# A two-layer hybrid decoder trunk with a mixture of experts: feature-major residual, more expert buffers, a shorter router chain, unrolled layers

## The chip, the cores and the metric

The kernel runs on one core of one Trainium2 chip. The metric is the device time of one execution in microseconds (us), as a median over runs; less is better. TensorE (PE in the profile) multiplies, VectorE (DVE), ScalarE (ACT) and GpSimd (POOL) work on elements, SyncE (SP) issues nearly all DMAs.

## The reference

The input is 256 tokens of 1024 features in fp32. Each of two layers does the following, and a final RMSNorm ends it:

```
h = rms_norm(x, norm_mix)
proj = h @ w_in                       # 1024 x 4120
y = [gated DeltaNet (6 heads) | retention (4) | mLSTM (6)], chunks of 64 in the reference
x = x + y @ w_out                     # 1024 x 1024
tok = rms_norm(x, norm_ffn)
group = top-1 of softmax(tok @ router_group)              # 4 groups
e1, e2 = top-2 of (tok @ router_expert + bias) in the group  # 8 experts each
weights = softmax(top two logits) * group probability
for e in range(32):
    y = (silu(tok @ gate[e]) * (tok @ up[e])) @ down[e]     # 1024 x 256, 1024 x 256, 256 x 1024
    out = out + combine[:, e] * y
x = x + out
```

An expert has three weight matrices of 1 MiB. One layer's experts are 96 such matrices, and every one is read in every layer.

## The kernel before

All of it is one function, `trunk`, with one program per engine; the engines meet by semaphores. The residual `x` lies token-major in SBUF: 128 partitions are tokens, two tiles `j` of 128 tokens, 1024 features along the free dimension. `hT` holds the normed input with features on partitions, in eight slices `k` of 256 tokens. Slice `k` holds every eighth feature from `k` on.

**A layer, in order.** (1) DVE scales `x` to `xn` (L1251), PE transposes it (L507), DVE evacuates with the gain (L1258) to `hT`. (2) The mixer: the projection is split into 20 weight slots (`PROJ`; `gatesT` at L523 is the first, the others go through L477 and L492), between them the work of the heads. (3) `project_out` (L784) multiplies by `w_out` in four parts `n`; DVE adds each to `x` (L1540, semaphore `x_mixed`). (4) The router: `x` is transposed (L834), `logitsT` is computed (L842), transposed back (L850), scaled by the row norm (L1559), then DVE picks group and experts in small instructions, each waiting for the one before (`link`). PE counts ranks (`rank`, L863 to L866); DVE builds `Psel`, a 0/1 matrix that picks 32 tokens for each of four experts (L1608). (5) The expert phase.

**Expert phase.** A quad is four experts. A round on PE is: gate matmuls of the quad (L912), transposed weights of the chosen tokens (L920), up matmuls (L912), the gather of the next round's tokens (`gather`, L881), transposes (L933), down matmuls (L942), and the combine into PSUM banks 0 to 3 (L953), where the residual has been put before by identity matmuls (L857). Eight quads, and a quad with more than 32 tokens for an expert gets another round (`nround`); the profiled execution has nine rounds in each layer. The gather must be exact in fp32: the normed tokens are split into three bf16 parts `part[0..2]` by ACT and POOL (L1192, L422, L1197, L425), and each is multiplied by `Psel`, 48 bf16 matmuls of 128x128.

**Loads.** SP issues each weight load in program order after waiting for `slots_free`, which PE raises when it has read a buffer. w_in and w_out take 24 loads in a ring of 12 buffers of 1 MiB. Experts take 96 loads in 16 buffers: the 12 of the ring and 4 (`SPARE`) in `shared`, memory that the mixer uses too. Loads come as gate, up, down of a quad, four each.

**Between layers.** The layers are a loop on each engine (`Fori(0, LAYERS)`); quads are a loop as well. At a layer's end all engines meet (`end_of_layer`), and POOL clears the layer's semaphores and lets them go on (L433). DVE copies the sums from PSUM to `x` (L1675), ACT squares them (L1219, L1222) for the next norm.

## Time and profile before

| what | value |
|---|---|
| median of 3 runs | 1034.73 us (1033.13 to 1035.6) |
| the profiled execution's own time | 1033.16 us |
| its span, first to last instruction | 1031.4 us |
| PE busy | 859.6 us (83%) |
| DVE busy | 347.2 us (34%) |
| ACT busy | 216.8 us (21%) |
| POOL busy | 23.0 us (2%) |
| mean granted TensorE clock | 0.939 |
| moved by DMA | 249.42 MB, mean 242 GB/s |

What lies around the span is 1.8 us. Busy time is an average over stages that have different limits: for each stage one reads which wait ended last.

### The profile page before, as it was taken

Reading aid. Unit: us, or ns where it says so; the run is one execution under the profiler, and the core shown is the slowest. Engines: PE = TensorE matmul, PEld = TensorE weight load, DVE = VectorE, ACT = ScalarE, POOL = GpSimd, SP = SyncE. Lnnn points to the kernel's source line nnn. Section 1 sums busy time; section 2 is a strip of 40 time slices with the busy share of each in tenths; the row PEclk is TensorE's granted clock in tenths of the full one; section 3 lists DMA queues with packets and bytes.
Section 4 is the critical chain, followed back from the end, with each engine's and each line's share of the span. In section 5 each row is a group of like instructions: output and inputs, shape, how many; then the busy total and the mean of one; then the engine's idle time right before and its main releaser. Section 6 shows DMA issues by size and latency. Waiting matters only on the chain.

```text
span 1031.4 us, 18112 instructions
## 1 busy us (share of the span) xinstructions
PE 859.6 (83%) x6932; PEld 617.0 (60%) x6933; DVE 347.2 (34%) x773; ACT 216.8 (21%) x410; POOL 23.0 (2%) x26
## 2 busy tenths in 40 slices
PE   4999999989588867698679999999896877879665
PEld 3877887968354433444358778879674544445332
DVE  1656634424621111111126565344346111111112
ACT  1243222222311100011103442133123111111111
POOL 1000000000300000000000000000003000000000
PEclk9999999989899888899879999999998998989888
DMA  9913012534459999979955120134344799899993
GB/s 343 350 57 103 1 42 82 167 119 163 169 244 419 421 420 421 421 323 421 403 207 183 42 82 1 45 119 163 107 172 157 306 420 421 337 423 419 420 421 138
DMA packets 48474, 249.42 MB, mean 242 GB/s; under 512 B 6096, under 2 KB 18560, under 8 KB 19344
## 3 DMA queue, kind: packets, MB, share of 16 engines
q1 hardware_dynamic: 47824, 246.91, 60.4%
q0 software_dynamic: 576, 1.43, 0.5%
q8 instruction: 58, 0.95, 0.4%
q14 instruction: 16, 0.13, 0.0%
HBM read 247.50 MB, written 1.05 MB: 241 GB/s over the span
## 4 chain that ended last, share of the span: by engine, by line
PE 50%; DMA 23%; DVE 12%; issue 7%; PEld 2%; ACT 2%; PEldq 1%; SPq 1%; DVEq 1%; POOLq 0%; ACTq 0%
PE ps L477 16%; DMA ring<-e_down 15%; PE ps L784 5%; PE ps L912 5%; PE ps L942 5%; DMA ring<-e_up 4%; PE ps L492 3%; PE ps L881 3%; DMA shared<-e_down 3%; DVE kq L1425 3%; DVE shared L1430 2%; PE ps L685 1%; PEld ps L912 1%; PE ps L639 1%; PE ps L953 1%
## 5 line engine op out<-in xcount | busy, mean ns | idle before, releaser
L477 PE MATMUL ps<-hT,ring 128*128 128x256 f32 x864 | 191.0, 381 | 0.0
L477 PEld LDWEIGHTS ps<-hT,ring 128*128 128x128 f32 x864 | 162.7, 190 | 25.9 <-issue 2.5
L912 PE MATMUL ps<-ring,hT 128*32 128x256 f32 x1728 | 114.7, 424 | 43.0 <-DMA ring<-e_up 21.7
L912 PEld LDWEIGHTS ps<-ring,hT 128*32 128x32 f32 x1728 | 67.2, 122 | 90.6 <-issue 69.8
L881 PEld LDWEIGHTS ps<-kq 128*128 128x128 bf16 x960 | 65.0, 149 | 10.0 <-issue 7.4
L953 PE MATMUL ps<-hT,kq 128*128 128x512 f32 x144 | 66.1, 602 | 5.5 <-PE ps L942 5.5
L881 PE MATMUL ps<-kq 128*128 128x128 bf16 x960 | 67.9, 235 | 2.3 <-DVE kq L1608 2.3
L1608 DVE TENSOR_TENSOR kq<-shapes,sel 128x128 bf16<-128x128 f32 (+1 forms) x40 | 9.9, 288 | 156.0 <-PE ps L920 155.7
L942 PE MATMUL ps<-ring,kq 128*32 128x512 f32 x448 | 51.0, 595 | 13.1 <-DMA ring<-e_down 8.4
L784 PE MATMUL ps<-ring,xn 128*128 128x256 f32 x256 | 58.8, 385 | 0.0
L912 PE MATMUL ps<-shared,hT 128*32 128x256 f32 x576 | 39.8, 437 | 21.9 <-DMA shared<-e_up 20.4
L953 PEld LDWEIGHTS ps<-hT,kq 128*128 128x128 f32 x144 | 25.9, 189 | 47.2 <-issue 47.2
L784 PEld LDWEIGHTS ps<-ring,xn 128*128 128x128 f32 x256 | 48.6, 193 | 7.9 <-issue 1.3
L912 PEld LDWEIGHTS ps<-shared,hT 128*32 128x32 f32 x576 | 22.0, 126 | 39.7 <-issue 32.4
L1212 ACT ACTIVATE kq<-ps 128x256 f32<-128x256 f32 x18 | 6.9, 384 | 181.6 <-PE ps L933 181.6
L1669 DVE TENSOR_TENSOR kq<-kq,ps 128x256 f32<-128x256 f32 x18 | 7.6, 421 | 101.9 <-PE ps L912 101.9
L1625 DVE TENSOR_TENSOR hT<-ps,par 128x512 f32<-128x512 f32 x40 | 27.7, 692 | 36.9 <-PE ps L881 36.6
L1672 DVE COPY hT<-ps 128x512 f32<-128x512 f32 x18 | 12.4, 692 | 80.0 <-PE ps L942 80.0
L942 PEld LDWEIGHTS ps<-ring,kq 128*32 128x32 f32 x448 | 14.8, 109 | 39.2 <-issue 33.2
L1208 ACT ACTIVATE kq<-ps 128x256 f32<-128x256 f32 x18 | 6.9, 384 | 147.0 <-PE ps L912 147.0
L492 PE MATMUL ps<-ring,hT 128*128 128x128 f32 (+1 forms) x256 | 36.4, 302 | 0.0
L492 PEld LDWEIGHTS ps<-ring,hT 128*128 128x128 f32 x256 | 34.4, 191 | 2.2 <-issue 0.3
(303 smaller groups left out, 976.9 us busy)
## 6 DMA issues: line engine op xcount, KB each, us to landing
ring<-e_gate SPq DMA_DIRECT2D x48, 1024.0 KB, 21.8
ring<-e_up SPq DMA_DIRECT2D x48, 1024.0 KB, 10.8
ring<-e_down SPq DMA_DIRECT2D x48, 1024.0 KB, 23.6
ring<-w_mix SPq DMA_DIRECT2D x34, 1024.0 KB, 10.1
shared<-e_down SPq DMA_DIRECT2D x16, 1024.0 KB, 7.8
shared<-e_gate SPq DMA_DIRECT2D x16, 1024.0 KB, 18.7
shared<-e_up SPq DMA_DIRECT2D x16, 1024.0 KB, 26.5
ring<-w_mix SPq DMA_DIRECT2D x12, 512.0 KB, 7.2
```

The lines of the kernel that those rows point to most:

```text
L477: mm = pe.matmul(bank[:, ct * T:(ct + 1) * T], w[:, k, ct * P:(ct + 1) * P], hT3[:, k, :], start=(k == 0), stop=(k == KD - 1))
L492: mm = pe.matmul(bank[:, j * n:(j + 1) * n], hT3[:, k, j * P:(j + 1) * P], w[:, k, 0:n], start=(k == 0), stop=(k == KD - 1))
L639: mm = pe.matmul(bank[0:rows_, m * P + c0:(m + 1) * P], Amat[:, 4 * g + m, 0:rows_], XT[:, 4 * g + m, c0:P], start=True, stop=True)
L784: mm = pe.matmul(ps[:, b, j * COLS:(j + 1) * COLS], mixT[:, k, j * P:(j + 1) * P], w[:, k, :], start=(k == 0 and j == 0), stop=(k == KD - ...
L881: mm = pe.matmul(ps[:, 4 + 3 * half, kk * P:(kk + 1) * P], part[i][:, j, k:D:KD], Psel[:, j, :], start=(j == 0 and i == 0), stop=(j == TT ...
L912: mm = pe.matmul(ps[32 * e:32 * e + 32, 5 + m, 0:DE], hq[:, k, 32 * e:32 * e + 32], slot[at[e]][:, k * DE:(k + 1) * DE], start=(k == 0), s ...
L942: mm = pe.matmul(ps[32 * e:32 * e + 32, 5 + h, :], hmT[:, f, 32 * e:32 * e + 32], slot[at[e]][:, f * D + h * 512:f * D + (h + 1) * 512], s ...
L953: mm = pe.matmul(ps[:, 2 * j + h, :], PwT[:, j * P:(j + 1) * P], ysb[:, h, :], start=False, stop=False, skip_group_check=True)
L1425: link(TTn(diag(h), src, lvl[:, lev, :].unsqueeze(1).to_broadcast([P, 2, P]), ALU.mult))
L1430: link(TTn(XT[r_, 4 * g:4 * g + 4, c0:P], XT[r_, 4 * g:4 * g + 4, c0:P], bank.rearrange("p (m t) -> p m t", m=4)[r_, :, c0:P], ALU.subtract))
L1625: TTn(hq[:, half * 4:half * 4 + 4, :], ps[:, 4 + 3 * half, :].rearrange("p (k s) -> p k s", k=4), gq[:, half * 4:half * 4 + 4].unsqueeze(2 ...
L1672: dve.tensor_copy(ysb[:, 1, :], ps[:, 6, :]).then_inc(y1_ready, 1)
```

## The change

1. **Feature-major residual.** `xT` holds the residual with features on partitions (weights and outputs are permuted on the host to fit). The norm of the mixer sums squares over features by a matmul with a tile of ones (`ssq`), and DVE makes `hT` by one instruction per `k`. The transposes of `xn` go. `project_out` has weights stationary. In layer 1 the experts' sums gather feature-major in PSUM too, in layer 2 token-major for the output.
2. **19 load buffers for experts:** 12 of the ring, `S0` to `S3` in `shared`, `K` in `kq`, `L` (`late_buf`), `X` (the memory of `xT`, lent once the residual has been put in PSUM). A host-side `load_plan` writes down buffer and wait of each load.
3. **Router.** Logits from `xT` directly, with the group logits padded to 8 columns so that the maximum reads them in place; squares summed by matmuls into the same bank; indices compared without a cast; the mask of experts made from two small one-hot parts; what only the weights need stands behind the mask.
4. **fp32 gather:** `xn` comes from four transposes of `xT`, scaled by ACT; 16 fp32 matmuls of 128x128 instead of 48 bf16; POOL does nothing in it.
5. **Layers and quads unrolled, no barrier.** Semaphores count on (`upto`), POOL clears nothing. Parameters of both layers come in one DMA at the start; the constants' DMA stands behind the first three weight loads.
6. **Norm from PSUM:** at a layer's end ACT squares the sums in PSUM into 128x1024 halves, and the last norm reads PSUM as well.

```diff
+    ring, freed, count, landed, plan = list(range(RING)), {}, 0, {}, []
+    for _ in range(LAYERS):
+        wide = ring[0:8] + ["S0", "S3", "S1", "S2", "K"] + ring[8:12] + ["L", "X"]
+        gone = [ring[i % RING] for i in range(NPROJ)] + wide[8:]
+        gone += [wide[m % len(wide)] for m in range(NMOE)]
...
-    banks = [i % 8 for i in range(len(order))]
+    banks = [(i + 4) % 8 for i in range(len(order))]
...
         def _(sync):
-            sync.dma_start(shapes[:, :], consts).then_inc(const_in, 16)
-            with sync.Fori(0, LAYERS) as l:
+            for l in range(LAYERS):
                 for i in range(NMIX):
+                    b, need, _ = loads[l][i]
+                    if need:
+                        sync.wait_ge(slots_free, need)
+                    sync.dma_start(slot[b][:, 0:n], w_mix[l, i, :, 0:n]).then_inc(arrived[b], 16)
+                    if l == 0 and i == 2:
+                        sync.dma_start(shapes[:, :], consts).then_inc(const_in, 16)
...
         def _(pool):
-                for j in range(TT):
-                    pool.wait_ge(part_ready, j + 1)
-                    pool.tensor_tensor(rest[:, j, :], xn3[:, j, :], part[0][:, j, :], ALU.subtract).then_inc(rest_ready, 1)
-                for j in range(TT):
-                    pool.wait_ge(part_ready, TT + j + 1)
-                    pool.tensor_tensor(part[2][:, j, :], rest[:, j, :], part[1][:, j, :], ALU.subtract).then_inc(rest_ready, 1)
-                pool.wait_ge(layer_end, l * 4 + 4)
-                pool.sem_clear(per_layer)
-                pool.sem_inc(layer_go, 1)
...
         def _(pe):
-                transpose_x("hT", 0)
-                pe.wait_ge(hT_ready, 4)
+                bank = begin("ssq")
+                for i in range(2):
+                    pe.wait_ge(squared, upto(l, squared, i + 1))
+                    for k in range(4):
+                        mm = pe.matmul(bank[:, 0:T], ones[:, :], sq_in[:, 4 * (i if l == 0 else 1 - i) + k, :],
+                                       start=(i == 0 and k == 0), stop=(i == 1 and k == 3))
                 for k in range(KD):
+                    pe.wait_ge(hT_ready, upto(l, hT_ready, k + 1))
                     mm = pe.matmul(bank[0:NG, 0:T], slot_w(0)[:, k, 0:NG], hT3[:, k, :], start=(k == 0), stop=(k == KD - 1))
...
-                for i in range(4):
-                    j, half = i // 2, i % 2
-                    bank = begin(("h2T", i))
-                    pe.wait_ge(x_mixed, 4)
-                    for kk in range(4):
-                        mm = pe.transpose(bank[:, kk * P:(kk + 1) * P], x[:, j, half * 4 + kk:D:KD], c("ident"))
+                for n in range(4):
+                    pe.wait_ge(x_mixed, upto(l, x_mixed, n + 1))
+                    for k in (2 * n, 2 * n + 1):
+                        mm = pe.matmul(bank[0:NLOG, 0:T], rw[:, k, :], xT[:, k, :], start=(k == 0), stop=(k == KD - 1))
+                for n in range(4):
+                    pe.wait_ge(squared, upto(l, squared, n + 3))
+                    for k in (2 * n, 2 * n + 1):
+                        mm = pe.matmul(bank[64:96, 0:T], ones[:, 0:32], sq_mid[:, k, :], start=(k == 0), stop=(k == KD - 1))
...
+                for i in range(4):
+                    j, half_ = i // 2, i % 2
+                    bank = begin(("xt", i))
+                    for kk in range(4):
+                        mm = pe.transpose(bank[:, kk * P:(kk + 1) * P], xT[:, half_ * 4 + kk, j * P:(j + 1) * P], c("ident"))
...
+                pe.wait_ge(acc_init, upto(l, acc_init, 1))
+                pe.sem_inc(slots_free, 1)
...
                             for j in range(TT):
-                                for i in range(3):
-                                    mm = pe.matmul(ps[:, 4 + 3 * half, kk * P:(kk + 1) * P], part[i][:, j, k:D:KD], Psel[:, j, :],
+                                mm = pe.matmul(ps[:, 4 + 3 * half_, kk * P:(kk + 1) * P], xn3[:, j, k * P:(k + 1) * P], Psel[:, j, :],
...
-                with pe.Fori(0, QUADS // LAP) as mlap:
-                    for u in range(LAP):
+                for q in range(QUADS):
...
-                end_of_layer(pe, l)
...
         def _(act):
+                    act.activation(sq_in[:, 4:8, :], ps[:, 2:4, :].rearrange("p b (k t) -> p (b k) t", t=T), ACT.Square).then_inc(squared, 1)
+                    act.wait_ge(x_out, upto(l - 1, x_out, 1))
+                    act.activation(sq_in[:, 0:4, :], ps[:, 0:2, :].rearrange("p b (k t) -> p (b k) t", t=T), ACT.Square).then_inc(squared, 1)
+                link(act.activation(rstd_row[:, :], bank[:, 0:T], ACT.Ln, scale=1.0 / D, bias=epsc[:, :]))
+                act.activation(rstd_row[:, :], rstd_row[:, :], ACT.Exp, scale=-0.5).then_inc(rstd_ready, 1)
...
         def _(dve):
-                scale_x()
-                evac_hT("hT", "gain_mix")
+                for k in range(KD):
+                    dve.scalar_tensor_tensor(out=hT3[:, k, :], in0=xT[:, k, :], scalar=pv(l, "gain_mix", k), in1=rstd_row[:, :],
+                                             op0=ALU.mult, op1=ALU.mult).then_inc(hT_ready, 1)
...
-                link(dve.tensor_copy(rt[:, :, 30:31], rtx[:, 0, :, 0:1]))
-                link(dve.tensor_copy(rt[:, :, 48:50], rtx[:, 1, :, 0:2]))
-                link(TTn(rt[:, :, 59:60], rt[:, :, 41:42], rt[:, :, 40:41], ALU.subtract))
+                link(TTn(oh[:, :, 0:2, :], iota[:, 0:PER_GROUP].unsqueeze(1).unsqueeze(1).to_broadcast([P, TT, 2, PER_GROUP]),
+                         rtx[:, 1, :, 0:2].unsqueeze(3).to_broadcast([P, TT, 2, PER_GROUP]), ALU.is_equal))
+                link(TTn(oh[:, :, 2, :], oh[:, :, 0, :], oh[:, :, 1, :], ALU.add))
+                link(experts(0, 2))
                 dve.sem_inc(mask_ready, 1)
```

**DVE in the router.** First the rows of before, from the second group index to the two expert casts (`rt` is a small scratch tile, `rtx` the indices, `pick` the masks); then the rows after, as far as the mask of experts.

```order
L1568 MAX_INDEX rtx<-rt 128x8
L1569 CAST rt<-rtx 128x2
L1570 TENSOR_TENSOR rt<-rt 128x2x4
L1572 TENSOR_TENSOR rt<-shapes,rt 128x2x4
L1576 TENSOR_TENSOR pick<-lg,rt 128x64
L1577 TENSOR_REDUCE rt<-pick 128x2x8
L1579 MAX rt<-rt 128x8
L1580 MAX_INDEX rtx<-rt 128x8
L1579 MAX rt<-rt 128x8
L1580 MAX_INDEX rtx<-rt 128x8
L1581 CAST rt<-rtx 128x2x2
L1582 TENSOR_TENSOR rt<-rt 128x2
```

```order
L1538 MAX_INDEX rtx<-rt,lg 128x8
L1539 TENSOR_TENSOR rt<-shapes,rtx 128x2x4
L1543 TENSOR_TENSOR pick<-lg,rt 128x64
L1544 TENSOR_REDUCE rt<-pick 128x2x8
L1546 MAX rt<-rt 128x8
L1547 MAX_INDEX rtx<-rt 128x8
L1546 MAX rt<-rt 128x8
L1547 MAX_INDEX rtx<-rt 128x8
L1548 TENSOR_TENSOR oh<-shapes,rtx 128x2x16
L1550 TENSOR_TENSOR oh<-oh 128x2x8
L1554 TENSOR_TENSOR pick<-rt,oh 128x64
```

Both casts and the two subtractions are gone from ahead of the mask; before, five more instructions (L1585 to L1594) follow L1582 until the mask stands, and after none follows L1554.

**PE in the router,** from the last part of `project_out` to the first gather, before and then after (layer 1).

```order
L834 MATMUL ps<-shapes,x 128x128 x16
L842 MATMUL ps<-hT,rw 36x256 x8
L850 MATMUL ps<-shapes,lgT 128x128 x2
L857 MATMUL ps<-x,shapes 128x512 x4
L863 MATMUL ps<-pick,shapes 128x64
L864 MATMUL ps<-pick,shapes 128x64
L866 MATMUL ps<-pick,shapes 128x32
L357 ISA
L881 MATMUL ps<-kq 128x128 x48
```

```order
L822 MATMUL ps<-xT,rws 40x256 x8
L826 MATMUL ps<-hT,ones 32x256 x8
L831 MATMUL ps<-shapes,lgT 128x128 x2
L838 MATMUL ps<-shapes,xT 128x128 x16
L844 MATMUL ps<-xT,shapes 128x512 x4
L856 MATMUL ps<-pick,shapes 128x64
L857 MATMUL ps<-pick,ones 128x64
L859 MATMUL ps<-pick,ones 128x32
```

The 16 transposes moved from ahead of the logits to behind them, ahead of the rank; eight matmuls with ones are new. The gather follows as `L872 MATMUL ps<-kq,xn 128x128 x16`.

## Rows read from the trace of the kernel before

**Rows 1.** The page: the chain that ended last, shares of the span by engine.

```profile
PE 50%; DMA 23%; DVE 12%; issue 7%; PEld 2%; ACT 2%; PEldq 1%; SPq 1%; DVEq 1%; POOLq 0%; ACTq 0%
```

**Rows 2.** Windows: stretch, its length, busy time by engine, clock, DMA share, GB/s.

```profile
340.00:370.00 30.00, 21.42 (x232) 11.88 (x228) 3.48 (x8) 3.00 (x5) 0.00 (x0) 0.85 1.01 420
437.00:450.00 13.00, 11.71 (x114) 5.08 (x118) 1.09 (x3) 2.60 (x4) 0.00 (x0) 1.00 0.60 250
```

**Rows 3.** Timeline of SP's queue, expert loads: start, duration of issue, what.

```profile
293.10 2.07 SPq L395 DMA_DIRECT2D ring<-e_up  x4
...
449.20 2.19 SPq L395 DMA_DIRECT2D ring<-e_up  x4
...
805.03 2.09 SPq L395 DMA_DIRECT2D ring<-e_up  x4
```

**Rows 4.** Timeline of PE, expert phases of both layers; in brackets the idle time before.

```profile
437.44 3.64 PE L942 MATMUL ps<-ring,kq 128*32 128x512 f32 x32 [1.12 <-DMA ring<-e_down]
...
453.19 3.16 PE L881 MATMUL ps<-kq 128*128 128x128 bf16 x48
...
461.06 3.67 PE L953 MATMUL ps<-hT,kq 128*128 128x512 f32 x8 [0.30 <-PE ps L942]
464.66 3.66 PE L912 MATMUL ps<-shared,hT 128*32 128x256 f32 x64
...
492.94 5.12 PE L912 MATMUL ps<-shared,hT 128*32 128x256 f32 x64 [4.37 <-DMA shared<-e_up]
...
503.17 3.64 PE L942 MATMUL ps<-ring,kq 128*32 128x512 f32 x32 [1.71 <-DMA ring<-e_down]
507.10 3.67 PE L953 MATMUL ps<-hT,kq 128*128 128x512 f32 x8 [0.29 <-PE ps L942]
...
1014.39 3.64 PE L942 MATMUL ps<-ring,kq 128*32 128x512 f32 x32 [1.69 <-DMA ring<-e_down]
```

**Rows 5.** Timeline of PE in the first router.

```profile
261.46 2.00 PE L834 MATMUL ps<-shapes,x 128*128 128x128 f32 x16 [1.13 <-DVEq L1542]
264.25 3.62 PE L842 MATMUL ps<-hT,rw 128*36 128x256 f32 x16 [0.78 <-ACT hT L1183]
...
268.76 3.66 PE L857 MATMUL ps<-x,shapes 128*128 128x512 f32 x8
279.93 0.66 PE L863 MATMUL ps<-pick,shapes 128*128 128x64 f32 x2 [7.50 <-DVEq L1595]
...
282.55 5.32 PE L881 MATMUL ps<-kq 128*128 128x128 bf16 x48 [1.17 <-DVE kq L1608]
289.04 3.66 PE L912 MATMUL ps<-ring,hT 128*32 128x256 f32 x64 [1.16 <-DVE hT L1625]
```

**Rows 6.** Timeline of all engines in the same stretch: DVE and POOL.

```profile
268.96 0.55 DVE L1559 SCALAR_TENSOR_TENSOR lg<-ps,ss,par 128x36 f32<-128x36 f32 x2 [0.65 <-PE ps L850]
...
272.72 0.17 DVE L1570 TENSOR_TENSOR rt<-rt 128x8 f32<-128x8 f32 x1
...
274.21 4.20 POOL L425 TENSOR_TENSOR kq<-hT,kq 128x1024 bf16<-128x1024 f32 x2 [1.55 <-ACT kq L1197]
...
276.39 2.04 DVE L1582 TENSOR_TENSOR rt<-rt 128x2 f32<-128x2 f32 x1
```

**Rows 7.** The chain that ended last, in time, between the layers: start, duration, what.

```profile
510.83 1.24 DVE x L1675
...
514.53 6.10 issue
...
526.63 5.32 PE ps L523 x16
```

**Rows 8.** Timeline at the start: first projection matmuls.

```profile
16.43 3.62 PE L523 MATMUL ps<-hT,ring 128*24 128x256 f32 x16 [1.46 <-DVEq L1260]
```

**Rows 9.** The chain in time: 16 fp32 matmuls of 128x128 (two instructions each).

```profile
203.64 3.57 PE ps L492 x32
```

**Rows 10.** The page, costliest groups: busy us, mean ns of one, idle before.

```profile
L1212 ACT ACTIVATE kq<-ps 128x256 f32<-128x256 f32 x18 | 6.9, 384 | 181.6 <-PE ps L933 181.6
```

More of the change, by code:

```diff
@@ L46 @@
 RING = 12
-SPARE = 4
 SLOT = 2048
@@ L101, with load_plan @@
 LN_EXP = "natural_log_exp_and_others"
+def load_plan():
+    ring, freed, count, landed, plan = list(range(RING)), {}, 0, {}, []
[3 more added lines that the diff above has]
+        gone += [wide[m % len(wide)] for m in range(NMOE)]
+        turns = {b: [freed[b]] if b in freed else [0] for b in ring}
+        for b in gone:
+            count += 1
+            freed[b] = count
+            turns.setdefault(b, []).append(count)
+        loads = []
+        for b in [ring[i % RING] for i in range(NMIX)] + [wide[m % len(wide)] for m in range(NMOE)]:
+            landed[b] = landed.get(b, 0) + 16
+            loads.append((b, turns[b].pop(0), landed[b]))
+        plan.append(loads)
+        ring = sorted(ring, key=lambda b: freed[b])
+    return plan
 def psum_plan():
-    order = [("hT", i) for i in range(4)] + ["gatesT", ("gdn", 0), "gates"] + [("gdn", s) for s in range(1, 5)]
+    order = ["ssq", "gatesT", ("gdn", 0), "gates"] + [("gdn", s) for s in range(1, 5)]
     order += ["rows", "cols", ("gate", 0), ("beta", 0), ("beta", 1)] + [("nrm", s) for s in range(3)] + [("gate", 1)]
@@ L259, in trunk @@
         ps = ctx.enter_context(nc.psum_tensor("ps", [P, 8, 512], F32))
-        first = sem("layer_first")
-        full = [sem(f"bank_full{b}") for b in range(8)]
-        free = [sem(f"bank_free{b}") for b in range(8)]
+        full = [sem(f"bank_full{b}", uses[b]) for b in range(8)]
+        free = [sem(f"bank_free{b}", uses[b]) for b in range(8)]
         dve_chain = sem("dve_chain")
         act_chain = sem("act_chain")
-        rstd_ready = sem("rstd_ready")
-        squared = sem("squared")
@@ new lines, in _ @@
+                for b in range(4):
+                    pe.wait_ge(free[b], upto(l, free[b], uses[b]))
+                if l + 1 < LAYERS:
+                    for n in range(4):
+                        mm = pe.matmul(ps[:, n, :], c("ident"), xT[:, 2 * n:2 * n + 2, :], start=True, stop=False, skip_group_check=True)
+                else:
+                    for j in range(TT):
+                        for k in range(KD):
+                            mm = pe.matmul(ps[:, 2 * j + k // 4, k % 4 * P:(k % 4 + 1) * P], xT[:, k, j * P:(j + 1) * P], c("ident"),
+                                           start=(k % 4 == 0), stop=False, skip_group_check=True)
@@ L865, in _ @@
                           skip_group_check=True)
-                mm = pe.matmul(bank[:, 64:96], c("ones"), pick[:, 0, 1, :], start=False, stop=True, skip_group_check=True)
+                mm = pe.matmul(bank[:, 64:96], ones[:, :], pick[:, 0, 1, :], start=False, stop=True, skip_group_check=True)
                 done(mm, "rank")
-                for b in range(4, 8):
-                    if b != bank_of["rank"][0]:
-                        pe.wait_ge(free[b], uses[b])
+                for b in (4, 5, 7):
+                    pe.wait_ge(free[b], upto(l, free[b], uses[b]))
@@ L1185, in _ @@
-                x_square(1)
-                act.wait_ge(hT_ready_act, 2)
-                for i in (1, 3):
-                    act.sem_inc(free[bank_of[("h2T", i)][0]], 1)
-                rstd(rstd_ready)
-                for j in range(TT):
-                    act.wait_ge(xn_ready, 3 + j)
-                    act.activation(part[0][:, j, :], xn3[:, j, :], ACT.Copy).then_inc(part_ready, 1)
-                act.wait_ge(route_in, 1)
+                for n in range(4):
+                    act.wait_ge(x_mixed, upto(l, x_mixed, n + 1))
+                    act.activation(sq_mid[:, 2 * n:2 * n + 2, :], xT[:, 2 * n:2 * n + 2, :], ACT.Square).then_inc(squared, 1)
@@ L1194, in _ @@
+                act.wait_ge(route_in, upto(l, route_in, 1))
                 act.activation(rt[:, :, 24:28], rt[:, :, 20:24], ACT.Exp).then_inc(route_exp, 1)
[L1195 to L1198 removed]
+                act.wait_ge(route_in, upto(l, route_in, 2))
                 act.activation(rt[:, :, 60:61], rt[:, :, 59:60], ACT.Exp).then_inc(route_exp, 1)
[L1200 removed]
@@ L1201, in _ @@
-                act.sem_inc(first, 1)
-                with act.Fori(0, QUADS) as q:
-                    act.reg_load(nreg, nround[0:1, bass.ds(q, 1)])
+                act.wait_ge(routed, upto(l, routed, 1))
+                for q in range(QUADS):
+                    act.reg_load(nreg, nround[0:1, q:q + 1])
                     nv = act.snap(nreg, min_val=1, max_val=MAXROUND)
@@ L1653, in _ @@
                 selected(n0)
-                with dve.Fori(0, QUADS) as q:
-                    dve.reg_load(nreg, nround[0:1, bass.ds(q, 1)])
+                for q in range(QUADS):
+                    dve.reg_load(nreg, nround[0:1, q:q + 1])
                     nv = dve.snap(nreg, min_val=1, max_val=MAXROUND)
```

873 lines of the change are left out of this document (406 added, 467 removed).

## The prediction

> **What bounds the kernel now.** I read the page first: PE holds half of the chain that ended last, DMA 23% [rows 1]. Such shares mix stages, so I took windows next. In the expert phase the DMA engines run full at 420 GB/s while PE is busy for 21.42 of 30 us [rows 2]: there the weights set the pace, and PE waits for them (4.37 and 1.71 us near the end of layer 1) [rows 4]. In the mixer it is the other way round, PE and the short DVE and ACT steps between its matmuls; loads wait for buffers. Between the two lies the router, a serial chain in which DVE takes small steps and PE idles for 7.50 us ahead of the rank [rows 5]. So three things count: how many expert loads are left when the phase begins, when it begins, and what stands between and ahead of the layers.
>
> A model of the loads first. A load of 1 MiB at 420 GB/s takes 2.50 us [rows 2]. From an empty queue, 20 loads are issued from 449.20 on and the last lands at 503.17, where the down matmuls start [rows 3, 4]: 53.97 = 4.0 + 20 x 2.50. So a phase from its first reissue to its last landing costs 4.0 + 2.50 per load, if the queue never runs dry. Before, 16 of 96 loads are in at the start, 80 remain: 204.0. The trace has 503.17 - 293.10 = 210.1 in layer 1 and 1014.39 - 805.03 = 209.4 in layer 2. The 6.1 and 5.4 too many are a dry queue: at the quad with two rounds PE keeps the gate buffers until its second gate pass (one combine, 3.67, behind the down matmuls at 437.44, and 3.66 long), and only then is the next load issued, 449.20; DMA is busy for 0.60 of 437 to 450 [rows 2 to 4].
>
> **The parts.** The sum is made against the profiled execution, 1033.16 us, which is 1.6 under the median of 1034.73.
>
> *Three more buffers.* Loads left are 77: 4.0 + 192.5 = 196.5, if the queue doesn't run dry. Does it? The second gate pass of that quad (loads 60 to 63) frees what load 79 needs. The down loads of the first round (up to 72) land 4.0 + 53 x 2.50 = 136.5 after the first reissue; PE frees the gates 449.20 - 437.44 = 11.8 later, at 148.3; the queue comes to load 79 at 60 x 2.50 = 150 or later. It just doesn't run dry; in layer 2 the same distances hold for an earlier quad, with the same 2 us to spare. The loan of xT comes once the residual is in PSUM, some 11 us ahead of the first reissue (below), enough for its load. So DMA's end moves by 13.6 and 12.9 us against the first reissue.
>
> Then PE may set the end. From the landing at 437.44 to the combine's end at 510.77 it needs 73.33 [rows 4]. Off go its waits, 4.37 and 1.71, and nothing else; each of its three gathers gets dearer by 0.41 (next item): 68.5. In layer 1 that makes 136.5 + 68.5 = 205.0 after the first reissue; by the loads it is 196.5 + 7.60 = 204.1. Before it was 510.77 - 293.10 = 217.7. **Gain 12.7 in layer 1.** In layer 2 the long quad comes earlier and loads decide: (1014.39 + 7.60 - 805.03) - 204.1 = **12.9**.
>
> *The fp32 gather.* 48 bf16 matmuls take 3.16 us [rows 4]. No fp32 gather is in the trace; the nearest row is 16 fp32 matmuls of the same 128x128 shape, 3.57 [rows 9]: +0.41. Bounds: no dearer than bf16, or at half pace, 7.1. Inside the phase it hides in layer 2 behind 30 us of loads per quad.
>
> The Trainium skill (FP8 and Floating Point Precision, TensorE Precision Notes) says that true fp32 makes four passes through the array, so 64 passes against 48, which speaks against the change: by pass count 3.16 would become 4.2. The row agrees in sign, not in size; by the page the total would be some 2 us more.
>
> *The router.* Before, lg is done at 268.96 + 0.55 [rows 6]. After: project_out ends, as before, when x_mixed 4 comes, 261.3, just before the transposes at 261.46 [rows 5]. PE is free from about 260.4, so eight logit matmuls (3.62 [rows 5]) run behind the four adds and end near 264.0, eight matmuls with ones of that kind near 267.6. That is no gain on 267.87, where logitsT ended before: the transposes saved pay for the squares. Copy and transposes as before; ACT's Ln and Exp of a 2-column tile now stand between: lg at 269.9, 0.4 later.
>
> Then DVE. Here the rows show something odd: a 128x2 subtraction takes 2.04 us, and its kind takes 0.17; it ends at 278.43, as does POOL's 4.20 from 274.21 [rows 6]. From lg at 269.5 to the mask at 279.8 it is 10.3, far more than 20 such steps would need. POOL does nothing now, so what remains costs its small price, about 0.20 with its gap and 0.25 for 64 columns: maximum and index four pairs at 0.47, six other steps, semaphore 0.14: 3.4. The mask stands at 273.3 and not 279.8.
>
> That is the Trainium skill's rule in SBUF — State Buffer, Who interferes with whom: a VectorE instruction with two SBUF inputs, or in a two-port mode, is blocked for a whole GpSimd instruction. By it too, every such step falls to its own price once POOL is idle; the trace agrees (2.04 against 0.17).
>
> But PE isn't free for the rank at 273.3. Moved ahead of it are 16 transposes (2.00) and the residual's matmuls (3.66) [rows 5], from 268.7 on: until 274.4. *This is what is late next:* the rank waits 1.1 us for PE. From rank to gather took 282.55 - 279.93 = 2.62; one DVE step less: 2.4 [rows 5]. Gather at 276.9, at full pace 3.57: 280.5 (before it ran at 5.32 for the same 48 that took 3.16 later, after PE had idled). DVE's steps for the weights and rounds stand ahead of the evacuations, 17 of about 0.23 (two masks, nine for the weights, two to weigh, four for the rounds), 4.0 us from 276.85: so the first evacuation starts at 280.9, not with the gather's first half, and the gate starts at 281.9. Before 289.04 [rows 5]. **Gain 7.1 in each layer, 14.2.** Bounds: if the casts saved still cost (mixed types 1 us), 5; without the wait for PE, 8.5.
>
> *Between the layers.* Before: sums done 510.83, first projection 526.63 [rows 7]: 15.8, of which 6.10 is DVE waiting for nothing shown, after the barrier, at the loop's start. After, from the end of the sums: ACT squares one half (about 1.1), DVE copies the other (1.24 [rows 7]), then ACT squares that, done at 2.4; eight matmuls with ones, four after each half, 0.45 each (3.62 for eight [rows 8]): done at 4.8; Ln and Exp of 128x256, 0.38 each with gaps [rows 10]: 5.8; first slice by DVE 0.45: PE starts at 6.4. The slices come at PE's own pace. **Gain 9.4.** Bounds 3.3 (the 6.10 stays, in code that is new each time) and 10.
>
> *The start.* Before 16.43 [rows 8]; PE waits for constants until 11.50, then transposes. After: the input is in by about 6.5, squares to 7.6, ones matmuls to 9.8, Ln, Exp and the first slice 1.5: 11.3. **Gain 5.0.** The constants, now behind 2.2 MB of weights, come some 6 us later, near 18; the gate transposes that need them start at 22. If parameters or they come later still, this term shrinks, at worst to 0.
>
> *The end.* The final norm reads PSUM without the copy of the sums, 1.24 [rows 7]: **gain 1.2**.
>
> *Between these, at nothing:* the mixers have the same instructions; banks are shifted by one, which moves waits at project_out by less than a DVE step either way. Semaphores without clearing cost nothing.
>
> Sum: 12.7 + 12.9 + 14.2 + 9.4 + 5.0 + 1.2 = 55.4. 1033.16 - 55.4 = 977.8; against the median 979.3. I say 979.
>
> **Rivals.** (a) *TensorE becomes the bound.* The gather takes 7.1 instead of 3.57. PE's end in layer 1 moves by 3 x 3.5 = 10.5, and each router's gather by 3.5: 996. For it: PE and DMA are within 1 us of each other at the end of layer 1. Against: [rows 9]. 0.12.
>
> (b) *The buffers don't pay.* The queue runs dry elsewhere, or loans come too late, so that the phase starts earlier but isn't shorter: 979 + 25.6 = 1005. For it: only 2 us to spare at the long quad. Against: even with the old gap, 7.5 us of loads are gone in each layer. 0.08.
>
> (c) *Slower: straight code isn't there in time.* Quads, written out, are new to each engine. If entering each of the 16 quads cost the 6.10 us of [rows 7] on PE's way, 97.6 would be lost: 1077. It decides from 55.4 / 16 = 3.5 us per quad. Against: PE already walks through four quads of written-out code per pass of its loop, and goes from a quad's combine (461.06 + 3.67) to the next one's gate at 464.66 without a gap [rows 4]. 0.04.
>
> The Trainium skill (Runtime: NRT & Kernel Launch, Instruction fetch mechanics) says that fetch is sequential and hidden, and that a taken branch out of its window stalls; by it the 6.10 goes with the loop, and (c) doesn't happen. The row at 514.53 fits, no row here shows the fetch itself.
>
> (d) *More than I sum:* the mixers' waits shrink by the shifted banks and the tail of each phase goes at full clock: 966. 0.06.
>
> **The numbers.** My forecast 0.70. The range has to leave out 2 in 10: (c) and part of (b) above, part of (d) below, and must take in the bounds of the boundary (+6) and the router (+4) together with (a): 965 to 1001. This kernel's measurement can tell about 0.2% from no change. Faster by more holds in all cases but (c): 0.95; within 0.01; slower 0.04.
>
> **What the profile after would show.** Right: first reissue of expert loads near 281 in layer 1 (start 5.0 earlier, router 7.1), 196 to 197 us from there to the last landing in each layer, DMA share 1.0 all through, no stretch at 0.6; gather of 16 at about 3.6; PE idle ahead of the rank only shortly; DVE's small steps all under 0.3; 6.4 us from the end of layer 1's sums to the next projection. Wrong: a stretch with DMA idle inside the phase (the 79th load); PE without waits over the last quads (the bound has changed); idle ahead of each quad on any engine; a late parameter DMA at the start.

## The result and the profile after

The changed kernel takes 977.09 us (median of 4 runs, 975.59 to 980.22), the kernel before 1035.13 us next to it. The ratio is 0.9444, 95% interval 0.9425 to 0.9463. The prediction was 979.0 (965 to 1001): right in sign, in size and in the range. The profiled execution, the longest of the four, took 980.22 us with a span of 978.2 us; before it was 1033.16 and 1031.4.

The page of the changed kernel, busy time by engine and the chain that ended last:

```profile
PE 871.0 (89%) x6740; PEld 641.3 (66%) x6740; DVE 325.5 (33%) x756; ACT 192.5 (20%) x385; POOL 4.3 (0%) x15
...
PE 61%; DMA 17%; DVE 10%; issue 5%; ACT 3%; SPq 2%; PEld 1%; PEldq 1%; DVEq 1%; ACTq 0%
```

DMA's share of the chain falls from 23 to 17%, that of DVE and of issue too [rows 1]; PE gets most of it. Shares mix stages, so I cut both spans at the same events: first projection, first reissue of an expert load, end of the sums. The expert phase after, in windows (stretch, its length, busy time by engine PE to POOL, clock, DMA share, GB/s):

```profile
340.00:370.00 30.00, 20.65 (x213) 12.90 (x212) 3.48 (x8) 1.71 (x4) 0.00 (x0) 0.89 1.01 421
...
433.00:450.00 17.00, 16.09 (x170) 10.90 (x174) 3.48 (x8) 1.23 (x3) 0.00 (x0) 1.00 1.01 421
```

The stretch in which DMA had stood at 0.60 [rows 2] is gone: 1.01 at 421 GB/s. The first router and the start of the expert phase (timeline of all engines: start, duration, what; in brackets the idle time before):

```profile
267.89 0.55 DVE L1529 SCALAR_TENSOR_TENSOR lg<-ps,ss,pars 128x40 f32<-128x40 f32 x2 [1.18 <-ACT ss L1173]
...
269.05 3.60 PE L844 MATMUL ps<-xT,shapes 128*128 128x512 f32 x8
...
271.69 0.22 DVE L1554 TENSOR_TENSOR pick<-rt,oh 128x64 f32<-128x64 f32 x1
...
272.37 0.16 DVE L1562 TENSOR_TENSOR rt<-rt 128x2 f32<-128x2 f32 x1
...
272.77 0.33 SPq L405 DMA_DIRECT2D xT<-e_up  x1
272.95 0.41 PE L856 MATMUL ps<-pick,shapes 128*128 128x64 f32 x2 [0.30 <-PE ps L844]
...
274.71 3.84 PE L872 MATMUL ps<-kq,xn 128*128 128x128 f32 x32 [0.94 <-DVE kq L1573]
...
278.74 1.29 DVE L1590 TENSOR_TENSOR hT<-ps,pars 128x512 f32<-128x512 f32 x2
...
280.03 3.66 PE L900 MATMUL ps<-ring,hT 128*32 128x256 f32 x64 [1.48 <-DVE hT L1590]
...
284.09 0.33 SPq L405 DMA_DIRECT2D ring<-e_up  x1
```

From lg to the gate it is 280.03 - 268.44 = 11.6, where it was 289.04 - 269.51 = 19.5 [rows 5, 6]. PE no longer idles 7.50 us ahead of the rank but 0.30. The 128x2 subtraction that took 2.04 [rows 6] takes 0.16. The boundary between the layers, in the chain that ended last (start, duration, what):

```profile
489.17 1.03 ACT xn L999
490.20 0.14 issue
490.34 3.71 PE ps L499 x16
...
494.07 0.48 ACT rowsraw L1003
...
494.66 0.42 ACT rowsraw L1005
...
495.18 0.50 DVE hT L1264
...
495.81 3.61 PE ps L507 x16
```

The sums end at 489.17 and the projection starts at 495.81: 6.6 instead of 15.8 [rows 7], and no row of 6.10 is left. The start, on PE:

```profile
6.12 6.49 PE L499 MATMUL ps<-xn,ones 128*128 128x256 f32 x16 [6.12 <-ACT xn L996]
...
14.42 3.61 PE L507 MATMUL ps<-hT,ring 128*24 128x256 f32 x16 [1.82 <-DVE hT L1264]
```

Here is the one term that is much too small: 16.43 [rows 8] becomes 14.42, not 11.3. The same eight matmuls with ones (16 instructions) that take 3.71 between the layers take 6.49 here. What the trace of before shows at its start:

```profile
11.50 3.48 PE L507 MATMUL ps<-shapes,xn 128*128 128x128 f32 x16 [11.50 <-DMA shapes<-consts]
```

The router's 16 transposes of the same shape take 2.00 [rows 5].

| stretch | before | after | gain | predicted |
|---|---|---|---|---|
| to the first projection | 16.43 | 14.42 | 2.0 | 5.0 |
| mixer and router, layer 1 | 276.7 | 269.7 | 7.0 | 7.1 |
| first reissue to end of sums, layer 1 | 217.7 | 205.1 | 12.6 | 12.7 |
| between the layers | 15.8 | 6.6 | 9.2 | 9.4 |
| mixer and router, layer 2 | 278.4 | 269.7 | 8.7 | 7.1 |
| first reissue to end of sums, layer 2 | 217.0 | 205.1 | 11.9 | 12.9 |
| end | 9.3 | 7.6 | 1.7 | 1.2 |
| sum | | | 53.1 | 55.4 |

The spans differ by 53.2. The row for the mixer of layer 2 holds 1.7 us that the prediction had at nothing: before, the first projection of layer 2 took 5.32 us [rows 7] at a mean granted clock of 0.68 (526.63 to 531.95), behind 10.90 us in which PE was idle and 16 transposes at 0.50. Now it follows a short wait and takes 3.61 at 1.00.

### The profile page after: what moved, and what is told of

Same layout as the page of the kernel before. It is cut to its first block, busy times and chain, and to the rows that moved or that the text cites. A ratio compares the mean times of both kernels' runs of the same rounds, so it can differ in the third digit from the quotient of the medians.

```text
span 978.2 us, 16745 instructions
## 1 busy us (share of the span) xinstructions
PE 871.0 (89%) x6740; PEld 641.3 (66%) x6740; DVE 325.5 (33%) x756; ACT 192.5 (20%) x385; POOL 4.3 (0%) x15
## 4 chain that ended last, share of the span: by engine, by line
PE 61%; DMA 17%; DVE 10%; issue 5%; ACT 3%; SPq 2%; PEld 1%; PEldq 1%; DVEq 1%; ACTq 0%
PE ps L469 17%; PE ps L900 8%; PE ps L771 5%; PE ps L930 5%; PE ps L872 4%; PE ps L484 4%; DMA ring<-e_down 3%; DMA ring<-e_up 3%; DMA xT<-e_gate 3%; DVE kq L1402 3%; DMA shared<-e_down 3%; DMA late_buf<-e_up 3%; DMA ring<-e_gate 2%; DVE shared L1407 2%; SPq L405 2%
## 5 line engine op out<-in xcount | busy, mean ns | idle before, releaser
L469 PE MATMUL ps<-hT,ring 128*128 128x256 f32 x864 | 193.8, 384 | 0.0
L469 PEld LDWEIGHTS ps<-hT,ring 128*128 128x128 f32 x864 | 164.9, 193 | 26.7 <-issue 2.5
L872 PEld LDWEIGHTS ps<-kq,xn 128*128 128x128 f32 x640 | 73.0, 192 | 9.9 <-issue 7.4
L872 PE MATMUL ps<-kq,xn 128*128 128x128 f32 x640 | 76.8, 278 | 2.2 <-DVE kq L1573 2.2
L771 PE MATMUL ps<-xn,ring 128*128 128x256 f32 x256 | 58.0, 382 | 0.0
L771 PEld LDWEIGHTS ps<-xn,ring 128*128 128x128 f32 x256 | 48.0, 190 | 7.5 <-issue 1.0
L1590 DVE TENSOR_TENSOR hT<-ps,pars 128x512 f32<-128x512 f32 x40 | 27.5, 691 | 46.4 <-PE ps L872 46.2
L900 PE MATMUL ps<-kq,hT 128*32 128x256 f32 x128 | 33.2, 418 | 4.4 <-DMA ring<-e_up 4.1
L900 PE MATMUL ps<-late_buf,hT 128*32 128x256 f32 x144 | 36.1, 409 | 0.3 <-DMA ring<-e_gate 0.2
L942 PEld LDWEIGHTS ps<-kq,hT 128*128 128x128 f32 x144 | 26.6, 190 | 14.0 <-issue 10.8
L942 PE MATMUL ps<-kq,hT 128*128 128x256 f32 x144 | 33.3, 384 | 2.8 <-PE ps L930 2.8
L946 PE MATMUL ps<-hT,kq 128*128 128x512 f32 x72 | 33.1, 602 | 2.8 <-PE ps L930 2.8
```

Of the source, the lines that this page charges most:

```text
L469: mm = pe.matmul(bank[:, ct * T:(ct + 1) * T], w[:, k, ct * P:(ct + 1) * P], hT3[:, k, :], start=(k == 0), stop=(k == KD - 1))
L771: mm = pe.matmul(ps[:, b, i * T:(i + 1) * T], w[:, k, i * P:(i + 1) * P], mixT[:, k, :], start=(k == 0 and i == 0), stop=(k == KD - 1 and ...
L872: mm = pe.matmul(ps[:, 4 + 3 * half_, kk * P:(kk + 1) * P], xn3[:, j, k * P:(k + 1) * P], Psel[:, j, :], start=(j == 0), stop=(j == TT - 1))
L900: mm = pe.matmul(ps[32 * e:32 * e + 32, 5 + m, 0:DE], hq[:, k, 32 * e:32 * e + 32], slot[w[e][0]][:, k * DE:(k + 1) * DE], start=(k == 0), ...
L942: mm = pe.matmul(ps[:, k // 2, k % 2 * T:(k % 2 + 1) * T], ysb[:, h, k % 4 * P:(k % 4 + 1) * P], PwT[:, 0:T], start=False, stop=False, ski ...
L946: mm = pe.matmul(ps[:, 2 * j + h, :], PwT[:, j * P:(j + 1) * P], ysb[:, h, :], start=False, stop=False, skip_group_check=True)
```

## The experiments

All ratios are against the kernel before, run on the same chip beside each.

**Do the three lent buffers shorten the phase?** Take them out of the order of load buffers, with the releases that go with them:

```diff
-        wide = ring[0:8] + ["S0", "S3", "S1", "S2", "K"] + ring[8:12] + ["L", "X"]
+        wide = ring[0:8] + ["S0", "S3", "S1", "S2"] + ring[8:12]
```

> The changed kernel with K, L and X taken out of the experts' buffers: 16 as before. Nothing else differs. If loads set the end of the expert phase as the prediction has it, 80 loads are left at the first reissue, 4.0 + 200 us, and the queue runs dry at the quad with two rounds again (about 6 us): last landing 210 us after the first reissue, the sums complete at 217 to 218 instead of the 205.06 of the changed kernel, in both layers. In all 25 us more: about 1002, ratio to before 0.968. Rival, the buffers do not pay and the phase is only earlier: no change against the changed kernel, 0.944. Rival, only the dry queue goes and the three loads are hidden anyway: 12 us more, 0.956.

Measured: 998.63 us, 0.9646 (0.9628 to 0.9665), 21.5 over the changed kernel where 25 were expected; both rivals (0.944 and 0.956) are out. From the first reissue to the end of the sums it takes 497.23 - 279.55 = 217.7 us in layer 1 and 217.1 in layer 2, the lengths of the kernel before. So the buffers give 12.6 and 12.0, and the rest of the change nothing on balance within the phase. The total moved by less because the rest of this kernel was quicker: between the two profiled executions, 17.3 us apart, the first reissue comes 4.5 us earlier and the mixer of layer 2 takes 267.0 and not 269.7, and 12.6 + 12.0 - 4.5 - 2.7 is 17.4 (why, below). A second kernel gives two of the three back (K and L, not X, the residual's buffer):

> The changed kernel without the loan of xT's memory (X): 18 buffers. By the model 78 loads are left, 4.0 + 195 + 7.6 = 206.6 us from the first reissue to the end of the sums, against 205.06; the long quad had 2 us to spare and now none, so up to 1 us of a dry queue. Layer 1 +1.5 to 2.5, layer 2 +1.5 to 3.0: 3 to 5.5 us more in all, about 981, ratio 0.948. Rival, the loan comes too late to be of use: no change. Rival, TensorE alone sets the end of layer 1: only layer 2 gets longer, by 2.5.

Measured: 979.38 us, 0.9459 (0.9442 to 0.9476), only 2.3 over all three where 3 to 5.5 were expected. Its runs (979.04 to 979.58) lie within those of the changed kernel (975.59 to 980.22), so the phases have to decide. The phases are 489.21 - 281.03 = 208.2 and 206.8, against 205.1 each. So the third buffer is worth 3.1 us in layer 1 (1.5 to 2.5 were expected) and 1.7 in layer 2. The first two carry most, as they also nearly close the gap at the two-round quad: in layer 1 DMA is busy for 0.25 of 430 to 435 and 0.60 of 435 to 440 with 16 buffers, for 0.72 and 1.00 with 18, and for 1.02 and 1.01 with 19.

**Is it POOL's work that slows the router?** The kernel before, with POOL's four subtractions taken out. With them gone, ACT's second copy is scaled by 0 and the gather reads the second part twice, so the tokens are gathered in bf16 precision only; no instruction of another engine is left out:

```diff
-                    pool.tensor_tensor(rest[:, j, :], xn3[:, j, :], part[0][:, j, :], ALU.subtract).then_inc(rest_ready, 1)
+                    pool.sem_inc(rest_ready, 1)
...
-                                    mm = pe.matmul(ps[:, 4 + 3 * half, kk * P:(kk + 1) * P], part[i][:, j, k:D:KD], Psel[:, j, :],
+                                    mm = pe.matmul(ps[:, 4 + 3 * half, kk * P:(kk + 1) * P], part[min(i, 1)][:, j, k:D:KD], Psel[:, j, :],
...
-                    act.activation(part[1][:, j, :], rest[:, j, :], ACT.Copy).then_inc(part_ready, 1)
+                    act.activation(part[1][:, j, :], rest[:, j, :], ACT.Copy, scale=0.0).then_inc(part_ready, 1)
```

> The kernel before, with GpSimd's four subtractions left out (semaphores kept) and ScalarE's second copy scaled by 0, so that tokens are gathered in bf16 precision only; the instructions of all other engines are the same in number. If GpSimd's operations are what holds VectorE's steps, then the copy L1565 (0.95), the casts L1569 (1.10) and L1581 (1.62) and the subtraction L1582 (2.04) each fall to about 0.2, the rank starts 5.0 us earlier, TensorE idles less ahead of the gather, which may run at full pace (3.2 instead of 5.3): 5 to 7 us in each layer, 10 to 14 in all, ratio 0.986 to 0.990. Rival, casts from uint32 cost 1 us or more by themselves: only L1565 and L1582 fall, 2.7 us a layer, ratio 0.995.

Measured: 1023.35 us, 0.9883 (0.9862 to 0.9905), 12.1 faster. Its router, all engines:

```profile
269.88 0.55 DVE L1559 SCALAR_TENSOR_TENSOR lg<-ps,ss,par 128x36 f32<-128x36 f32 x2 [0.65 <-PE ps L850]
...
271.73 0.17 DVE L1569 CAST rt<-rtx 128x2 f32<-128x2 uint32 x1
...
274.17 0.16 DVE L1582 TENSOR_TENSOR rt<-rt 128x2 f32<-128x2 f32 x1
...
275.83 0.41 PE L863 MATMUL ps<-pick,shapes 128*128 128x64 f32 x2 [2.50 <-DVEq L1595]
...
277.83 4.62 PE L881 MATMUL ps<-kq 128*128 128x128 bf16 x48 [1.17 <-DVE kq L1608]
...
283.61 3.66 PE L912 MATMUL ps<-ring,hT 128*32 128x256 f32 x64 [1.16 <-DVE hT L1625]
```

The same instruction L1582 falls from 2.04 [rows 6] to 0.16 with only POOL's work gone, PE's idle time ahead of the rank from 7.50 to 2.50, and lg to gate from 19.5 to 283.61 - 270.43 = 13.2. Of the 7.9 that the changed kernel gains on that distance, 6.3 are POOL's silence; all else in the router adds 1.6 on balance (the mask comes 1.7 sooner behind lg, 3.5 against 5.2). The rival, casts that are slow by themselves, is out: the cast L1569 takes 0.17 and not 1.10. The trace of before shows it step by step too. POOL's four subtractions of 2.12 us end at 270.58, 272.66, 276.33 and 278.41; the four slow DVE steps L1565, L1569, L1581 and L1582 end at 270.60, 272.69, 276.36 and 278.43, each 0.02 to 0.03 us behind one of them. By the Trainium skill (SBUF — State Buffer, Who interferes with whom) that is the shared port pair; this run agrees, 2.04 against 0.16.

**What of the 15.8 between the layers was the meeting of the engines?** The changed kernel, with a meeting of PE, ACT and DVE after layer 1's sums, in straight code:

```diff
+                if l == 0:
+                    pe.sem_inc(layer_end, 1)
+                    pe.wait_ge(layer_go, 1)
```

> The changed kernel with a meeting of all engines between the two layers by two semaphores over GpSimd, as before, but in straight code, without a loop and without clearing semaphores. If the 6.10 us of the kernel before belong to the jump back to the loop's start, the meeting costs 0.3 to 1.5 us: from the sums complete to the first projection 7 to 8 us instead of 6.66. If the meeting itself costs them: about 12.5, 6 us more in all.

Measured: 975.66 us, 0.9421 (0.9404 to 0.9438), no different from the changed kernel. The chain at the boundary:

```profile
489.15 0.03 POOLq L427
...
489.20 1.03 ACT xn L1006
...
490.37 3.71 PE ps L503 x16
...
495.83 1.24 PE ps L511 x5
```

489.20 to 495.83 is 6.63, as without it. The meeting itself costs some 0.1 us here; none of the three engines has other work at that point. In the kernel before, with POOL's clearing of semaphores in it, the meeting took 0.6 (513.80 to 514.39 on the chain). So what the change saves at the boundary is for the most part not the meeting but what stood around it: the 6.10 at the loop's start, the transposes and the copies. No kernel here tried the loop without the meeting, so the 6.10 is put down to the loop only by its place. That straight code costs nothing of that size is measured: in layer 1's expert part PE's idle time ahead of gate or up matmuls for which nothing is shown is 1.8 us in six places, 0.4 at most.

**Why does the start give 2 and not 5?** My theory was a TensorE that is slow in its first microseconds. Twelve matmuls on a tile of ones are put ahead, while the input is still on its way:

```diff
+                    for _ in range(WARM):
+                        pe.matmul(ps[:, 0, 0:P], ones[:, :], ones[:, :], start=True, stop=True)
```

> The changed kernel as it is, on the same chip as the three that follow, as their reference: 0.944 of before.

> The changed kernel with 12 matmuls of the tile of ones by itself, into a bank that is overwritten later, ahead of the first sum of squares. They fill TensorE's time while the input is loaded. In the changed kernel the eight matmuls of the sum of squares at the start take 6.49 us; the same eight between the layers take 3.69. If that is TensorE's lower clock after idling, they now take 3.7, and the first projection starts 2.5 to 3 us earlier, near 11.6 instead of 14.42; everything behind moves with it: 2.5 to 3 us less in all. Rival, the input's DMA or the weight load sets that pace: still 6.5, no change.

The changed kernel again took 975.83 us, 0.9429 (0.9407 to 0.9452); the warmed one 974.11, 0.9413 (0.9388 to 0.9438). PE in the warmed kernel:

```profile
1.03 5.48 PE L495 MATMUL ps<-ones 128*128 128x128 f32 x24 [1.03 <-POOL epsc L416]
...
6.30 3.65 PE L502 MATMUL ps<-xn,ones 128*128 128x256 f32 x16
...
11.77 1.45 PE L510 MATMUL ps<-hT,ring 128*24 128x256 f32 x6 [1.82 <-DVE hT L1267]
```

After 5.3 us of work the eight matmuls take 3.65, not 6.49 or 6.15 (the two executions of the changed kernel), and the projection starts at 11.77. That is 0.5 beyond the 11.3 that I had predicted. The input came as before (ACT's second square ends at 7.45 and at 7.50), so the rival, its DMA, is out, and the missing microseconds are those matmuls at a slower pace. The windows print 1.00 for the granted clock there only for want of a record, so no row shows the level. The first clock record of a trace, at full clock, begins at 11.78 in the changed kernel, 9.11 in the one with 16 buffers (whose eight matmuls take 5.17) and 6.36 in the warmed one: the sooner it begins, the shorter the eight. The Trainium skill (TensorE: Matmul & The Clock Gate, What's actually happening) lists 1.2 GHz as the level of an engine that has been idle, which agrees with a factor of 6.49 / 3.65 = 1.8.

The total moved by less than the start, 1.7 us against 2.3, and the runs of the two overlap, so it stays unclear. Of the warmed kernel's six runs the two with a mean granted clock of 0.963 took 977.8 and 978.2, the other four (0.970 to 0.974) 972.3 to 975.2; the profile is of one of the two. What the clock does can be read in the windows of ten microseconds between 20 and 280. First the changed kernel, its first execution (only stretches below full clock), then one of these stretches in its second:

```profile
90.00:100.00 10.00, 8.20 (x43) 6.70 (x40) 6.86 (x13) 4.13 (x7) 0.00 (x0) 0.83 0.28 106
...
210.00:220.00 10.00, 7.34 (x42) 5.28 (x42) 3.63 (x8) 2.41 (x6) 0.00 (x0) 0.83 0.59 211
220.00:230.00 10.00, 10.00 (x56) 7.31 (x56) 2.25 (x6) 2.19 (x5) 0.00 (x0) 0.83 0.01 2
```

```profile
90.00:100.00 10.00, 7.89 (x54) 6.70 (x51) 6.86 (x13) 5.76 (x9) 0.00 (x0) 1.00 0.30 106
```

In the first execution PE is granted 0.50, that is 1.2 GHz, from 93.7 to 97.1, behind 1.80 us in which it was idle. In the second it is idle for the same 1.80 and keeps the full clock. The eight matmuls of a projection that follow (L469, 16 instructions) take 5.04 us in the first and 3.62 in the second. Summed as (1 - clock) x 10 over these windows, and beside it the time from first projection to first reissue in layer 1:

| execution | clock lost, us | mixer and router, us |
|---|---|---|
| 16 buffers | 0 | 266.5 |
| changed, second | 1.7 | 267.6 |
| 18 buffers | 3.4 | 267.8 |
| changed, first | 5.1 | 269.7 |
| with the meeting | 5.1 | 269.6 |
| warmed | 5.1 | 270.3 |

The more clock is lost, the longer the mixer. So the warmed kernel's profile gave its 2.3 back in the mixer, 270.3 against 267.6. That it is the clock can be read by laying the changed kernel's two executions side by side. The first is 0.32 us behind the second at the first projection and still at L596 (89.14 and 88.82), 1.49 behind it past the stretch at 95 (L626, 100.43 and 98.94), still 1.49 at L723 (213.28 and 211.79), and 2.31 past the stretch at 220, which lasts 6.8 us in the first and 3.4 in the second (L771, 224.36 and 222.05). So nearly all of the 2.1 us arises where the first execution had less clock.

**How near is TensorE to being the bound?** The gather matmuls issued twice:

```diff
-                        for kk in range(4):
+                        for kk in (0, 1, 2, 3, 0, 1, 2, 3):
```

> The changed kernel with the gather matmuls of every expert round issued twice (the second set writes the same part of PSUM again, so no value changes): 3.84 us more on TensorE in the router round and in each of the seven later rounds of a layer. My theory (the loads set the end up to the last rounds, in which layer 1 of the changed kernel shows TensorE without waits for a DMA): 3.8 us more in each router (7.7 together), and in the expert part what the last rounds that no longer wait for loads cannot hide. In layer 1 TensorE's work ends 0.9 us behind the loads' bound, and the last three rounds show no wait for a load, so 7 to 12 us; layer 2 shows PE waiting for loads to the end (6.06 us in the last quads), so 0 to 6. Together 15 to 26 us over the changed kernel's 977.1, i.e. 992 to 1003, ratio 0.958 to 0.969. Rival 1, the loads cover every extra gather: only the routers pay, 983 to 986, ratio 0.950 to 0.952. Rival 2, the rival of the prediction in which TensorE is the bound over the whole expert part: 8 x 3.84 x 2 = 61 us more, 1038, ratio 1.00.

Measured: 1005.55 us, 0.9704 (0.9685 to 0.9723), 28.5 over the changed kernel and above my 15 to 26. The phases grow from 205.1 to 505.46 - 283.90 = 221.6 and to 997.86 - 785.48 = 212.4. PE's waits in layer 1 (engine, what waited for what: us in total, times, longest), first the changed kernel, then this one:

```profile
PE ps L900 <- DMA ring<-e_gate: 6.4, 3, 3.9
PE ps L900 <- DMA ring<-e_up: 5.8, 1, 5.8
PE ps L900 <- DMA shared<-e_up: 4.4, 1, 4.4
PE ps L900 <- DMA late_buf<-e_up: 4.1, 1, 4.1
...
PE ps L930 <- DMA shared<-e_down: 0.8, 1, 0.8
PE ps L930 <- DMA ring<-e_down: 0.7, 1, 0.7
```

```profile
PE ps L900 <- DMA shared<-e_up: 5.0, 1, 5.0
...
PE ps L900 <- DMA late_buf<-e_up: 3.2, 1, 3.2
```

Three things in my expectation were off. A doubled gather costs a router only 2.0 and not 3.8 (from the gather to the gate 279.84 - 272.50 = 7.34, against 5.32), because DVE's steps for the weights stand there anyway. There are nine later gathers in a layer's phase, not seven: 9 x 3.57 = 32.1 us of added work (a doubled gather takes 7.41 where one takes 3.84). And the loads cover much less than I thought: in layer 1 the waits for loads shrink from 22.2 to 8.2, so 14.0 is hidden and 18.1 should show, measured 16.5. In layer 2 they shrink from 21.9 to 2.4, so 12.6 should show, and 7.3 does. There the granted clock of the phase rose from 0.95 to 0.99: PE waits less, and so spends less time at 1.2 GHz behind its waits. The 64 up matmuls of a quad take 6.06 right behind a wait of 4.10, at a mean granted clock of 0.59, and 3.66 without. PE's busy time in the phase grows by 200.34 - 175.50 = 24.8 for the 32.1 of added work, so the other matmuls took 7.3 less. So in the changed kernel TensorE and DMA are nearly level over the whole phase, with some 22 us of play per layer, of which a part is eaten by the lower clock.

**Can the two microseconds ahead of the rank, and those behind it, be had?** The last quarter of the residual's matmuls is put behind the rank, DVE's evacuations go between its steps for the weights, and the round counts ahead of them:

```diff
+                residual((0, 1, 2))
...
+                residual((3,)).then_inc(acc_init, 1)
```

> The changed kernel with its router reordered: on TensorE three quarters of the residual's matmuls stand ahead of the rank and one quarter behind it (where TensorE idles for 0.94 us); on VectorE the round counts come right behind the first selection, and the evacuations of the gather are put between the steps for the weights. Nothing is added or left out. The rank no longer waits for TensorE (0.9 us), and the gate starts right behind the gather instead of 1.48 us later: 2.3 us in each layer, 4.6 in all. Rival, the weights then come too late for the transposes behind the gate, so that half is given back: 2.3 in all. Rival, the end of each phase does not follow its start: no change.

Measured: 970.89 us, 0.9383 (0.9359 to 0.9406), 4.9 under the changed kernel's 975.83 on the same chip; their runs don't overlap (969.82 to 973.59 against 974.95 to 977.71). Its router:

```profile
265.85 0.55 DVE L1534 SCALAR_TENSOR_TENSOR lg<-ps,ss,pars 128x40 f32<-128x40 f32 x2 [1.18 <-ACT ss L1178]
...
270.08 0.41 PE L858 MATMUL ps<-pick,shapes 128*128 128x64 f32 x2 [0.33 <-DVEq L1564]
...
271.84 3.84 PE L875 MATMUL ps<-kq,xn 128*128 128x128 f32 x32
...
273.93 0.69 DVE L1595 TENSOR_TENSOR hT<-ps,pars 128x512 f32<-128x512 f32 x1 [0.29 <-PE ps L875]
...
275.61 3.66 PE L905 MATMUL ps<-ring,hT 128*32 128x256 f32 x64
```

From lg to the gate it takes 9.2, against 11.6: the rank now starts 0.2 behind the mask, not 1.0, and the first evacuation follows the gather's first half, 2.1 after the gather begins instead of 4.0. Twice 2.4 is 4.8. Both edits together, this order and the warm-up:

> Both edits, warm TensorE at the start and the reordered router: 7 to 7.6 us less than the changed kernel, about 970, if each is worth what it is alone.

Measured: 969.51 us, 0.9371 (0.9348 to 0.9394), the lowest median of the study, 6.3 under the changed kernel's 975.83 beside it and so less than expected. Between this and the one before it (968.19 to 972.05 against 969.82 to 973.59) the runs can't decide.

## Why the prediction was right, step by step

*The model of the loads* held. In layer 2 the last up load that PE waits for lands at 952.23, 186.7 after the first reissue; 4.0 + 73 x 2.50 is 186.5. The chain at the end of that layer:

```profile
924.97 27.26 DMA ring<-e_up
...
952.37 6.06 PE ps L900 x64
...
962.91 3.69 PE ps L930 x32
```

The queue never ran dry, so the 2 us to spare at the long quad were enough, and xT's loan at 272.77 came 11.3 ahead of the first reissue ("some 11").

*Layer 1*: PE was to set the end at 205.0; measured 205.1. The last wait for a load is where the sum had it, at the down matmuls of the two-round quad's first round:

```profile
421.19 0.59 PE L930 MATMUL ps<-shared,kq 128*32 128x512 f32 x1 [0.66 <-DMA ring<-e_down]
```

That is 137.1 after the first reissue (136.5 in the sum), and the rest takes 68.0 (68.5). By this the prediction's list of signs contradicts its own sum: "PE without waits over the last quads" stands there as a sign of being wrong, and the sum rests on it in layer 1. *Layer 2*: 204.1 was predicted and 205.1 came. The step was that loads decide there. They decide only up to the last up load: behind its wait PE runs the up matmuls in 6.06, not 3.66, and so reaches the down matmuls 962.91 - 952.37 = 10.5 later, when the four down loads (10.0) are in. So in both layers PE ends the phase.

*The gather*: 3.84 against 3.57 predicted and 3.16 before. Rival (a) with its 7.1 is out as stated. The doubled gather, at 7.41, shows that it was priced too low: 996 was said, 1005.55 came, for the rival counted three gathers of layer 1 and in the trace 16.5 us of nine show, and 7.3 more in layer 2. By the Trainium skill's rule of four passes (FP8 and Floating Point Precision, TensorE Precision Notes) the estimate was 4.2; the trace lies between, 0.4 below it and 0.3 above the row's 3.57.

*The router*, by its distances: lg to mask 3.5 (predicted 3.4), mask to rank 1.0 (1.1), rank to gather 1.8 (2.4), gather to first evacuation 4.0 (4.0), evacuation to gate 1.3 (1.0). The prediction's "what is late next", PE with the residual's matmuls, is what the trace shows, and the reordered kernel takes it away.

*Between the layers*: 9.2 for 9.4, nearly each piece as written. *The end*: 1.7 for 1.2.

*The start* is the failed step. "Ones matmuls to 9.8" priced eight matmuls with rows from the middle of the run, where PE had been busy; at 6 us it had done nothing, and they took until 12.6. The rest of the term was right within 0.5. The warning stood in the trace of before: its first 16 transposes took 3.48 and not 2.00. So the first reissue came at 284.09 and not at 281.

*Mixers at nothing* left out the 1.7 us that the first projection of layer 2 gets back from the clock (rows 7 had its 5.32). For the rest it is right within what the clock does: 2 us between two executions of one program. That much of the close match is luck: layer 1 gives 7.0 for 7.1 in the profiled execution and would give 9.1 in the second one (267.6). In the sum, too, misses of both signs offset each other: -3.0 at the start and -1.0 in the loads of layer 2, +1.6 in its mixer and +0.5 at the end.

*The rivals*: (b) is out, by the kernels with 16 and 18 buffers: the buffers pay 12.6 and 12.0. (c) is out: PE begins no quad behind more than 0.4 us that nothing explains. (d), 966, was not reached.

## What to carry to other kernels

When loads bound a phase, count them from the first reissue and price each at its bytes over the measured rate; then ask what the other engine needs from the last landing on, at the clock that it has behind a wait. A buffer can be worth more than its own load if it closes a gap in the queue, and the next one less: here two of the three gave 9.5 of 12.6 us in layer 1 and 10.3 of 12.0 in layer 2. Before a serial chain of small DVE steps is shortened, look at what POOL is doing meanwhile: silence gave 6.3 of 7.9 us. Price the first matmuls of a kernel, and those behind a long idle time, by rows that stand in the same place and not by rows from the busy middle.
